# Recurrence scores on four array quarters, and attention projections as three-product groups

## What is computed

```python
def step(s, inp):
    r_t, w_t, kk_t, a_t, k_t, v_t = inp
    s_kk = jnp.einsum('bhvk,bhk->bhv', s, kk_t)
    s = (s * w_t[:, :, None, :] - s_kk[..., None] * (kk_t * a_t)[:, :, None, :]
         + v_t[..., None] * k_t[:, :, None, :])
    return s, jnp.einsum('bhvk,bhk->bhv', s, r_t)
```

## Time and profile before

| | us |
|---|---|
| median of 3 runs | 3371.77 (3365.54 to 3376.61) |
| the profiled execution | 3371.36 |
| its span | 3369.7 |
| PE busy | 2928.1, 87%, 30053 matmul records |
| PE weight loads busy | 2329.7, 69% |
| DVE busy | 1900.6, 56% |
| ACT busy | 1347.0, 40% |
| POOL busy | 536.5, 16% |
| mean granted TensorE clock | 0.936 of full speed |

### The profile page before, as it was taken

One profiled execution on the slowest core, in us unless ns is written; L12 is line 12 of the kernel. 1 busy time (PEld: TensorE's weight loads), 2 busy tenths in 40 slices (PEclk: granted clock), 3 DMA queues, 4 the chain that ended last, 5 costly groups with the idle time before them and its releaser, 6 DMA issues. The chain is left out here.

```text
span 3369.7 us, 69659 instructions
## 1 busy us (share of the span) xinstructions
PE 2928.1 (87%) x30053; PEld 2329.7 (69%) x30053; DVE 1900.6 (56%) x3045; ACT 1347.0 (40%) x2016; POOL 536.5 (16%) x489
## 2 busy tenths in 40 slices
PE   7998789898999569999456999999939987769999
PEld 3563678878879458887336999999924334548877
DVE  4431565566665246765746888888860035446652
ACT  1002445545454232221225777777720126423331
POOL 3001434545542010000000000000010026200000
PEclk8999999999999689999778999999969979889999
DMA  4543000000000147655109999999812111112222
GB/s 189 215 150 105 19 4 20 20 20 20 20 3 4 75 154 295 262 200 196 66 27 370 371 369 367 364 371 367 318 56 101 57 33 34 50 67 96 94 105 77
DMA packets 73484, 483.06 MB, mean 143 GB/s; under 512 B 11075, under 2 KB 12483, under 8 KB 31728
## 3 DMA queue, kind: packets, MB, share of 16 engines
q1 hardware_dynamic: 58832, 418.48, 33.3%
q0 software_dynamic: 12096, 52.43, 4.1%
q10 hardware_dynamic: 2304, 8.39, 0.6%
HBM read 457.73 MB, written 34.13 MB: 146 GB/s over the span
## 5 line engine op out<-in xcount | busy, mean ns | idle before, releaser
L2156 DVE TENSOR_TENSOR sb_moe_w_lo<-w_ring,sb_moe_w_hi 128x1408 fp32r<-128x1408 f32 (+1 forms) x132 | 255.2, 1934 | 67.8 <-ACT sb_moe_w_hi L2110 67.2
L2056 PE MATMUL ps<-sb_moe_w_hi,sb_x_feat_lo 128*128 128x352 f32 x832 | 274.1, 329 | 11.5 <-DVE sb_moe_w_lo L2156 11.5
L2058 PE MATMUL ps<-sb_moe_w_hi,sb_x_feat_hi 128*128 128x352 f32 x832 | 268.2, 322 | 0.0
L2057 PE MATMUL ps<-sb_moe_w_lo,sb_x_feat_hi 128*128 128x352 f32 x832 | 267.6, 322 | 0.0
L2110 ACT ACTIVATE sb_moe_w_hi<-w_ring 128x2816 fp32r<-128x2816 f32 x80 | 204.2, 2554 | 0.1
L2056 PEld LDWEIGHTS ps<-sb_moe_w_hi,sb_x_feat_lo 128*128 128x128 f32 x832 | 156.8, 189 | 17.3 <-issue 17.3
L2056 PE MATMUL ps<-sb_moe_w_hi,sb_hid_feat_lo 128*128 128x256 f32 x572 | 163.1, 285 | 3.9 <-DVE sb_hid_feat_lo L2182 3.9
L2058 PE MATMUL ps<-sb_moe_w_hi,sb_hid_feat_hi 128*128 128x256 f32 x572 | 161.8, 283 | 0.0
L2057 PE MATMUL ps<-sb_moe_w_lo,sb_hid_feat_hi 128*128 128x256 f32 x572 | 161.8, 283 | 0.0
L231 PE MATMUL ps<-sb_conv_hl,sb_hi_conv 128*128 128x512 f32 x352 | 140.0, 398 | 22.9 <-DVE sb_lo_conv L219 22.9
L231 PE MATMUL ps<-sb_ffn_features,sb_hi_ffn 128*128 128x512 f32 x352 | 140.1, 398 | 22.1 <-DVE sb_lo_ffn L219 22.1
(11 more groups left out here) (501 smaller groups left out, 7816.7 us busy)
## 6 DMA issues: line engine op xcount, KB each, us to landing
w_ring<-w_moe_up SPq DMA_DIRECT2D x67, 1408.0 KB, 8.3
sb_hm<-w_ada SPq DMA_DIRECT2D x48, 1024.0 KB, 6.9
w_ring<-w_ffn SPq DMA_DIRECT2D x22, 1024.0 KB, 4.8
w_ring<-w_up SPq DMA_DIRECT2D x22, 1024.0 KB, 4.9
...
```

The source lines that it names most:

```text
L2056: pe.matmul(out, x_lo, w_hi, start=first, stop=False)
L2057: pe.matmul(out, x_hi, w_lo, start=False, stop=False)
L2058: return pe.matmul(out, x_hi, w_hi, start=False, stop=end)
L2156: return V.tensor_tensor(WL[:, s, w], raw[raw_at(c, i)[0]][:, w], WH[:, s, w].bitcast(F32), ALU.subtract)
```

## The change

Two changes together.

**In `pairs`.** `trans` is gone as an item of its own; its products are part of `score`. Products of FB with FA and FR, and the turns of FA and FB, stay on the two own quarters and go to bank i (columns 0 to 255 and 256 to 511). Products of FK, and the turns of FK and v, go from row half hh to the other column half and land in bank 4. So the score of a chunk issues products on all four quarters. ACT copies in two pieces: `trO` (128x256 from bank 4) and, after DVE's `LKE`, `trE` (128x256 from bank i). DVE masks in two: `LKE` from bank i and, after `trO`, `LKO` from bank 4. Score n waits for `trO` and `LKO` of chunk n-1 and for `akA` of n-4.

`akv` is split. `akA` (4 products into bank i, an ACT copy of 128x128) stands for all four chunks of the quad before ahead of its first score; `akO` (8 products in a context chunk, 12 in a latent one, on the crossed quarters, into bank 5) stands between scores and includes the parts with v that Z and Y had. `Z` has 4 products, `Y` 8, and Z stands ahead of Y. On DVE stand `pre` (held part + state, both in SBUF), two `ends` (times the decay, SBUF to SBUF, 128x64 each, after a semaphore on `pre`), then two `z` (PSUM times decay plus that), and for latent chunks `Y` (PSUM + held part), which was ACT's.

The number of products is the same: 108 in a latent chunk and 88 in a context chunk, level phase included.

**In `qkv`.** One block in place of two. `Stream` gets a parameter `up`; 12 chunks (8 of w_qk, 4 of w_v) run through it, each split into high and low parts by ACT and DVE, and H is split into HH and HL first. Each fp32 product becomes a group of three fp32r products. The sums lie on four column tiles (partitions 32j to 32j+31 of bank 0), the spreads on four row tiles into four banks; they stand between the value chunks, the last eight behind them. Squares are taken as 128x1024 into H. The bias table's and lambda's work moves behind chunks 2 and 4.

The diff, cut to its core:

```diff
+out += [(pp, f"akA{n}") for n in prev]
 for i in range(4):
     out += [(p, f"score{n}") for n in cur[i:i + 1]]
-    out += [(pp, f"akv{n}") for n in prev[i:i + 1]]
-    out += [(p, f"trans{n}") for n in cur[i:i + 1]]
+    out += [(pp, f"akO{n}") for n in prev[i:i + 1]]
...
-links += [[(pp, f"U{n}")], [(pp, f"Y{n}")] * lat(n) + [(pp, f"Z{n}")] * (n < NCH - 1)]
+links += [[(pp, f"U{n}")], [(pp, f"Z{n}")] * (n < NCH - 1) + [(pp, f"Y{n}")] * lat(n)]
...
 if n == CCH:
     pe.wait_ge(f_pool.sem, f_pool.at("R", p))
 if n >= 4:
-    pe.wait_ge(act_f.sem, act_f.at(f"t{LAST}.{n - 4}", p))
+    pe.wait_ge(act_c.sem, act_c.at(f"akA{n - 4}", p))
...
 if n == 0:
     pe.wait_ge(s_v[u], 16 * (p // 2 + 1))
 if n:
-    pe.wait_ge(act_f.sem, act_f.at(f"tr{n - 1}", p))
+    pe.wait_ge(act_f.sem, act_f.at(f"trO{n - 1}", p))
+    pe.wait_ge(dve_f.sem, dve_f.at(f"LKO{n - 1}", p))
...
 for d in range(2):
-    for o, src in enumerate((FA[:, d, at(d)], FK[:, d, at(d)], v[:, at(d)], FB[:, d, at(d)])):
-        for hh in heads:
-            to = 256 * d + o * CH
-            last = pe.matmul(ps[hh, 4, to:to + CH], src[hh], ident[hh, hh], start=True, stop=True)
+    for half in range(1 + lat(n)):
+        to = d * P + half * CH
+        for hh, oo in both_ways:
+            x_in = FR[hh, d, chunk_at(n, d) - CTX:chunk_at(n, d) - CTX + CH] if half else FA[hh, d, at(d)]
+            pe.matmul(ps[hh, i, to:to + CH], FB[hh, d, at(d)], x_in, start=True, stop=True)
+        for hh, oo in both_ways:
+            x_in = FR[hh, d, chunk_at(n, d) - CTX:chunk_at(n, d) - CTX + CH] if half else FA[hh, d, at(d)]
+            pe.matmul(ps[oo, 4, to:to + CH], FK[hh, d, at(d)], x_in, start=True, stop=True)
+    for o, (own, other) in enumerate(((FA[:, d, at(d)], FK[:, d, at(d)]), (FB[:, d, at(d)], v[:, at(d)]))):
+        to = 256 + d * P + o * CH
+        for hh, oo in both_ways:
+            pe.matmul(ps[hh, i, to:to + CH], own[hh], ident[hh, hh], start=True, stop=True)
+        for hh, oo in both_ways:
+            last = pe.matmul(ps[oo, 4, to:to + CH], other[hh], ident[hh, hh], start=True, stop=True)
...
+    for d in range(2):
+        for hh in heads:
+            last = pe.matmul(ps[hh, i, d * CH:(d + 1) * CH], tr[hh, 0, d, 0, :], tb[hh, d, 1, :],
+                             start=True, stop=True)
+elif head == "akO":
+    pe.wait_ge(dve_f.sem, dve_f.at(f"LKO{n}", p))
     if n % 4:
-        pe.wait_ge(act_c.sem, act_c.at(f"akv{n - 1}", p))
+        pe.wait_ge(act_c.sem, act_c.at(f"akO{n - 1}", p))
     elif n:
-        pe.wait_ge(dve_c.sem, dve_c.at(f"z{n - 1}", p))
+        pe.wait_ge(dve_c.sem, dve_c.at(f"Y{n - 1}" if lat(n - 1) else f"z{n - 1}", p))
     elif p:
         pe.wait_ge(act_c.sem, act_c.at(f"U{NCH - 1}", p - 1))
+        pe.wait_ge(dve_c.sem, dve_c.at(f"Y{NCH - 1}", p - 1))
     for d in range(2):
-        for hh in heads:
-            pe.matmul(ps[hh, 5, d * CH:(d + 1) * CH], M[hh, d, 2, :], tr[hh, d, 2, :], start=True, stop=True)
...
+to = d * CH
+for hh, oo in both_ways:
+    pe.matmul(ps[hh, 5, to:to + CH], M[oo, 1, d, 0, :], tr[oo, 1, d, 1, :], start=True, stop=True)
+for hh, oo in both_ways:
+    last = pe.matmul(ps[hh, 5, P + to:P + to + CH], tr[oo, 1, d, 0, :], tr[oo, 1, d, 1, :],
                      start=True, stop=True)
+if lat(n):
+    for hh, oo in both_ways:
+        last = pe.matmul(ps[hh, 5, 2 * P + to:2 * P + to + CH], tr[oo, 1, d, 1, :], M[oo, 1, d, 1, :],
+                         start=True, stop=True)
...
 elif head == "Z":
     pe.wait_ge(act_c.sem, act_c.at(f"U{n}", p))
     for d in range(2):
         to = 3 * P + d * CH
         for hh in heads:
-            pe.matmul(ps[hh, 5, to:to + CH], tr[hh, d, 1, :], tr[hh, d, 2, :], start=True, stop=False)
-        for hh in heads:
-            last = pe.matmul(ps[hh, 5, to:to + CH], tr[hh, d, 3, :], Us[hh, d, :], start=False, stop=True)
+            last = pe.matmul(ps[hh, 5, to:to + CH], tr[hh, 0, d, 1, :], Us[hh, d, :], start=True, stop=True)
...
-if head == "trans":
+if head == "score":
     act.wait_ge(pe_f.sem, pe_f.at(x, p))
-    S.activation(TR[:, s, i].rearrange("p d o n -> p (d o n)"), ps[:, 4, :],
-                 ACT.Copy).then_inc(*act_f.did(f"tr{n}"))
+    S.activation(TR[:, s, i, 1].rearrange("p d o n -> p (d o n)"), ps[:, 4, 256:512],
+                 ACT.Copy).then_inc(*act_f.did(f"trO{n}"))
+    act.wait_ge(dve_f.sem, dve_f.at(f"LKE{n}", p))
+    S.activation(TR[:, s, i, 0].rearrange("p d o n -> p (d o n)"), ps[:, i, 256:512],
...
 if head == "score":
+    halves_in = slice(0, 2) if lat(n) else slice(0, 1)
     dve.wait_ge(pe_f.sem, pe_f.at(x, p))
-    by = 1 if lat(n) else 2
-    V.tensor_tensor(LK[:, s, i, :, ::by, :], ps[:, i, :].rearrange("p (d o n) -> p d o n", d=2, o=4)[:, :, ::by, :],
-                    mC[:, :, ::by, :], ALU.mult).then_inc(*dve_f.did(f"LK{n}"))
+    V.tensor_tensor(LK[:, s, i, 0, :, halves_in, :],
+                    ps[:, i, 0:256].rearrange("p (d o n) -> p d o n", d=2, o=2)[:, :, halves_in, :],
+                    mC[:, :, halves_in, :], ALU.mult).then_inc(*dve_f.did(f"LKE{n}"))
+    dve.wait_ge(act_f.sem, act_f.at(f"trO{n}", p))
+    V.tensor_tensor(LK[:, s, i, 1, :, halves_in, :],
+                    ps[:, 4, 0:256].rearrange("p (d o n) -> p d o n", d=2, o=2)[:, :, halves_in, :],
+                    mC[:, :, halves_in, :], ALU.mult).then_inc(*dve_f.did(f"LKO{n}"))
...
+elif head == "U" and n < NCH - 1:
+    dve.wait_ge(act_c.sem, act_c.at(f"akO{n | 3}", p))
+    held = AT[:, i, 2]
+    if n:
+        dve.wait_ge(dve_c.sem, dve_c.at(f"z{n - 1}", p))
+        V.tensor_tensor(Zs[:, :, :], held, Zb[:, n % 2, :, :], ALU.add).then_inc(*dve_c.did(f"pre{n}"))
+        dve.wait_ge(dve_c.sem, dve_c.at(f"pre{n}", p))
+        held = Zs
+    for d in range(2):
+        c = chunk_at(n, d) // CH
+        last = V.tensor_scalar(Zs[:, d, :], held[:, d, :], PE2[:, u, d, c:c + 1], None, ALU.mult)
+    last.then_inc(*dve_c.did(f"ends{n}"))
 elif head == "Z":
     dve.wait_ge(pe_c.sem, pe_c.at(x, p))
-    b = ps[:, 5, 3 * P:4 * P].rearrange("p (d n) -> p d n", d=2)
-    if n:
-        V.tensor_tensor(Zs[:, :, :], b, Zb[:, n % 2, :, :], ALU.add).then_inc(*dve_c.did(f"sum{n}"))
-        dve.wait_ge(dve_c.sem, dve_c.at(f"sum{n}", p))
-        b = Zs[:, :, :]
-    end = PE2[:, u, 0, chunk_at(n, 0) // CH:chunk_at(n, 0) // CH + 1]
-    step = NCH + (chunk_at(n, 1) - chunk_at(n, 0)) // CH
-    last = V.tensor_tensor(Zb[:, (n + 1) % 2, :, :], b,
-                           AP(end.tensor, end.offset, [end.ap[0], (step, 2), (0, CH)]), ALU.mult)
+    dve.wait_ge(dve_c.sem, dve_c.at(f"ends{n}", p))
+    for d in range(2):
+        c = chunk_at(n, d) // CH
+        last = V.scalar_tensor_tensor(out=Zb[:, (n + 1) % 2, d, :], in0=ps[:, 5, 3 * P + d * CH:3 * P + (d + 1) * CH],
+                                      scalar=PE2[:, u, d, c:c + 1], in1=Zs[:, d, :], op0=ALU.mult, op1=ALU.add)
     last.then_inc(*dve_c.did(f"z{n}"))
...
+V.tensor_tensor(AP(y.tensor, y.offset, [y.ap[0], (step, 2), (1, CH)]),
+                ps[:, 4, 0:P].rearrange("p (d n) -> p d n", d=2), AT[:, i, 3], ALU.add).then_inc(
+                    *dve_c.did(x))
...
-sp.dma_start(tab[0:33, :], A["bias_table"]).then_inc(s_b[0], 16)
-sp.dma_start(oh[0:33, :], A["bucket_onehot"]).then_inc(s_b[0], 16)
-load_chunks(sp, ring, A["w_qk"], 8, 2 * KT * P)
-sp.wait_ge(s_b[2], 2)
-sp.dma_start(A["bias_rows"], row[0:12, :]).then_inc(s_b[3], 16)
+for c in range(ALL):
+    s, trip = c % SLOTS, c // SLOTS
+    sp.wait_ge(ring.used[s], ring.used_at(s, trip - 1))
+    sp.dma_start(ring.buf[s][:, 0:2 * KT * P], A["w_qk"][c] if c < NQ else A["w_v"][c - NQ]).then_inc(
+        ring.loaded[s], 16)
+    if c == 1:
...
+def three(out, x_hi, x_lo, w_hi, w_lo, first, end):
+    pe.matmul(out, x_hi, w_lo, start=first, stop=False)
+    pe.matmul(out, x_lo, w_hi, start=False, stop=False)
+    return pe.matmul(out, x_hi, w_hi, start=False, stop=end)
...
+def squares(lo, hi):
+    for i in range(lo, hi):
+        j = 32 * (i % 4)
+        last = pe.matmul(ps[j:j + 32, 0, :], sums[:, i, :], SQ[:, i % KT, :], start=(i < 4), stop=(i >= 12))
+    last.then_inc(s_sum, 1)
+
+def spreads(lo):
+    for i in range(lo, lo + 4):
+        j = 32 * (i % 4)
+        if i >= 4:
+            pe.wait_ge(s_nn, i - 3)
+        pe.matmul(ps[:, i % 4, :], spread[j:j + 32, i, :], R[j:j + 32, :], start=True, stop=True).then_inc(s_sp, 1)
...
+values(NQ, range(TT)).then_inc(ring.used[NQ % SLOTS], 1)
+pe.wait_ge(s_sel, 80)
...
+squares(0, KT)
+pe.wait_ge(flow.w_lo, NQ + 2)
+values(NQ + 1, range(TT)).then_inc(ring.used[(NQ + 1) % SLOTS], 1)
...
+squares(KT, 2 * KT)
+pe.wait_ge(flow.w_lo, NQ + 3)
+pe.wait_ge(s_vo, 1)
+values(NQ + 2, range(TT)).then_inc(ring.used[(NQ + 2) % SLOTS], 1)
+pe.wait_ge(s_rec, 1)
+pe.wait_ge(ring.drained[1], ring.drained_at(1, 2))
+spreads(0)
+pe.wait_ge(flow.w_lo, NQ + 4)
+values(NQ + 3, (0, 1))
+spreads(4)
+values(NQ + 3, (2, 3)).then_inc(ring.used[(NQ + 3) % SLOTS], 1)
+spreads(8)
+spreads(12)
```

(3 more changed lines are left out.)

275 lines of the change are left out of this document (147 added, 128 removed).

## The result

The changed kernel takes 3408.6 us (median of 4 runs, 3405.3 to 3411.0) against 3371.4: a ratio of 1.011, 95% interval 1.0091 to 1.0130. It is slower by 37 us; forecast were 46 less and a range up to 3385. The profiled execution has a span of 3409.4, against 3369.7.

What follows compares the result with a forecast made beforehand. The prediction took PE to bound both changed stages, recurrence and attention's projections. From 3371.4 us, attention's -61 and the recurrence's +15 (-4 + 10 - 9 - 13 + 31) gave 3325, range 3262 to 3385.

Steps and rivals of the forecast that it cites:

- the port: Links: DVE's SBUF-to-SBUF `pre` and `ends` wait for running POOL operations to end, +31 us in third-quad level phases.
- turnaround -4: Fronts: waiting for bank 4's release takes almost all the four-quarter gain; latent period 2.27 us against 2.33, leaving -4.
- features +10: Fronts: features in ACT's and DVE's queues, such as a reciprocal, delay the next score; 1.3 us a pair, +10.
- links -9: Level phase: fewer Z and Y products save at most 4.7 us a pair; a quarter taken, 1.2 a pair, -9.
- L1335's other stalls -13: Recurrence: removing L1335 saves its waits for POOL outside the third quad, 1.6 us a pair, -13.
- the walk: Third quad's four links, `pre` and `ends` each waiting for POOL: level phase 20.8 to 28 us, +7.2 a pair, +50.
- factor of 0.6: Third quads' level phases: share taken of the +50 us for waits on POOL, since L1335 lost less than expected; +31.
- Four quarters: Scores and turns: all four array quarters work at once, saving 10.2 us a pair, 82 in all, as upper bound.
- Rival B: Recurrence: `ends` finds the port free or POOL's gaps suffice, shorter links show; gains 10 to 66 us, 3270; chance 0.33.
- Rival C: Recurrence: four quarters give nothing beyond 29.2 ns a record, merged scores still wait for bank 4; +79, 3398; chance 0.12.
- Attention: Projection block: three-product groups at 0.69 us against 0.858, sums and spreads on tiles; 222.5 to 161 us, -61.
- Case D: Tiles give attention nothing (-45) and the port costs the whole 50; 3373 us, no change; chance 0.10.

Runs made afterwards that it cites:

- one_ends: The changed kernel with the two tensor_scalar instructions of `ends` made one tensor_tensor of 128x128: 3368.8 us, 1.0006 against the kernel before.
- two_quarters: The changed kernel with old-state scaling on ACT, held part added by PE, and crossed products on their own quarters: 3379.9 us, 1.0030 against the kernel before.
- aka_both: The changed kernel with ACT scaling old state, PE adding held part, akA 1-3 behind scores 0-2, no feature among akA: 3330.8 us, 0.9882 against before.
- attn_act_ends: The kernel before with the change's attention block, ACT scaling the old state and z reading PSUM, without L1335: 3289.4 us, 0.9762 against the kernel before.
- attn_only: The kernel before with the change's attention block alone, old recurrence kept: 3306.0 us, 0.9823 against the kernel before.

## Why the prediction was wrong

The recurrence's +15 against its +103, term by term. The measured side adds up the stretches of all eight pairs; the akA are taken out of the level phases at 0.93 us a quad and put beside the fronts, where the forecast had them.

| us | forecast | measured |
|---|---|---|
| third quads' level phases of seven pairs (the port) | +31 | +75 |
| fronts and akA (turnaround -4, features +10) | +6 | +35 |
| first score's wait for ACT's copy of akA | 0 | +11 |
| all the rest (links -9, L1335's other stalls -13) | -22 | -18 |
| sum | +15 | +103 |

- **The port** is the step that failed first. The sentence was that the walk, `pre` and `ends` "each waiting for the operation that then runs", gives +7.2 a pair "and charges too much", so +31. It gave +12 beside the akA in each of the six middle pairs. Two things were mis-sized. `ends` is two instructions, and each lost a whole POOL operation (one_ends: 6.7 us less in that stretch). And the factor of 0.6, from L1335's mean, was wrong in kind: L1335 comes alone and meets POOL by chance, while the second and third of three instructions in a row come exactly when POOL has just taken its turn. The 13 us for L1335's stalls outside the third quads were a wrong reading too: in a middle pair it lost 4.0 us in the third quad and only 0.4 elsewhere, not 1.6. The clock fell with PE's pauses, which no term had, some 4 us of PE's work a third level phase.
- **The turnaround** was right as a mechanism and near in its period, but its term is the second step that failed: fronts with their akA were to cost +0.8 us a pair and cost +4.0. Scores follow each other after 2.20 us against 2.04 and after 1.85 against 1.65 in context fronts, 2.1 us a pair that the 0.14 for three hand-overs lacks; and behind the last score X0 waits for the last LKE, LKO and the transpose.
- **The akA's copy.** I counted their 0.23 a chunk on PE, but not that the first score waits for ACT's copy of the first one, behind a table load and an exponential: 1.77 us in the second quad of a pair. This is the step "ACT's and DVE's queues now stand on that path", applied to trO and LKO and not to akA.
- **The links** were under-counted as a gain, as far as the last pair shows, which has no POOL streak and no features of a next pair: from X0 to the end of the last T its third level phase took 15.9 us against 19.0, and without their akA the first and second took 0.8 and 0.9 less, 4.9 in all where I took 1.2. Up to 2.0 of these are L1335's own losses to POOL in that phase of the kernel before, so the links are worth 3 to 5 a pair there. In the middle pairs only the first level phase shows them in its length, 1.5.
- **Four quarters** was right: 64 records in 0.93 us, 14.6 ns each; two_quarters shows what they are worth in the period. Rival B is out with a third level phase of 33.8 us. Rival C is out, and with it the estimate by the Trainium skill's "TensorE: Matmul & The Clock Gate", section "Wait — 56ns, not 53.3ns?": records on different quarters start 6 to 8 ns apart in the trace. (By C's own sum that estimate is +52, 3377, and not +49.)
- **Attention** was right in size and by its steps: block 162.1 against 161, chunks 11.20 against 11.0, sums and spreads on tiles side by side.
- **The sign** did not follow from one term. 3325 with 75 for the port in place of 31 is 3369, no change; with the fronts' +35 it is 3398, with the wait for akA 3409, and the rest brings 3413, where the profiled run took 3411. Case C, the only one to end slower, was another mechanism; no case held the port at more than its walk, which the text itself called an over-charge. Case D held the walk's whole 50 but left out its own -4 and -9.

What stays open: aka_both and attn_act_ends have both the port out of the links and attention's part, and still differ by 41 us (4.7 us a pair: 1.9 in the third front, 0.9 in the first, 1.4 and 1.2 in the second and third stretches, 0.7 the other way in the first stretch). In aka_both the scores wait 24.1 us for copies of akA, which attn_act_ends does not have, and in the third front ACT stands ahead of trO as shown; how the rest divides was not tried. Nor was it tried why the first stretch is 1.7 us longer with ACT's scaling in it (29.4 in attn_act_ends, 27.7 in attn_only); that ACT's queue is fuller there is a guess.
